# Hybrid decoder layer on Trainium2: chunk matrices of the RWKV-7 mixing as 64-wide quarters, with the loop over head pairs written out

## The reference

```python
def step(st, inp):
    r_t, w_t, k_t, v_t, kk_t, a_t = inp
    sa = jnp.einsum('bhvk,bhk->bhv', st, kk_t)
    st = (st * w_t[:, :, None, :]
          - sa[..., None] * (kk_t * a_t)[:, :, None, :]
          + v_t[..., None] * k_t[:, :, None, :])
    y = jnp.einsum('bhvk,bhk->bhv', st, r_t)
    return st, y
```

## Time and profile before

| | |
|---|---|
| median of 3 runs | 1986.58 us (1986.14 to 1987.74) |
| profiled execution | 1987.96 us, its span 1986.2 us |
| granted TensorE clock, mean | 0.909 |
| TensorE, VectorE, ScalarE, GpSimd busy | 89%, 74%, 54%, 16% of the span |
| DMA | 456.72 MB |

### The profile page before, as it was taken

How to read it: one execution, slowest core, us unless ns; L and a number is a source line. 1 busy time by engine, 2 the same in 40 slices (tenths; PEclk the granted TensorE clock), 3 DMA queues, 4 the chain that set the end, 5 groups by cost and what they waited for, 6 DMA issues and landing times. The chain is left out here.

```text
span 1986.2 us, 26691 instructions
## 1 busy us (share of the span) xinstructions
PE 1771.6 (89%) x8812; PEld 1454.7 (73%) x8813; DVE 1465.4 (74%) x1291; ACT 1063.3 (54%) x979; POOL 308.7 (16%) x206
## 2 busy tenths in 40 slices
PE   6996978868695968999999999999999999999963
PEld 5884756747475856888888888888888888888851
DVE  3225646466664456998999989989989999999845
ACT  4233122122111345777777777777777777777731
POOL 6000000000000000221221222222212212222200
PEclk9997867859687978999999999999999999999985
DMA  5330000000001266999999999999999999999915
GB/s 158 95 96 15 1 1 3 0 3 0 0 0 41 100 240 257 345 363 361 355 363 364 358 369 358 362 369 348 356 370 346 360 367 347 363 359 353 360 69 224
DMA packets 98151, 456.72 MB, mean 230 GB/s; under 512 B 13152, under 2 KB 40816, under 8 KB 48400
## 3 DMA queue, kind: packets, MB, share of 16 engines
q1 hardware_dynamic: 87664, 435.93, 57.8%
q0 software_dynamic: 10464, 20.50, 2.8%
HBM read 452.71 MB, written 20.97 MB: 238 GB/s over the span
## 5 line engine op out<-in xcount | busy, mean ns | idle before, releaser
L1385 DVE TENSOR_TENSOR w_pieces_lo<-w_pieces,w_pieces_hi 128x2048 fp32r<-128x2048 f32 x384 | 870.8, 2288 | 103.8 <-ACT w_pieces_hi L1287 103.7
L1287 ACT ACTIVATE w_pieces_hi<-w_pieces 128x2048 fp32r<-128x2048 f32 x384 | 736.7, 1919 | 310.0 <-PE psum L1535 238.1
L1532 PE MATMUL psum<-w_pieces_hi,xh 128*128 128x512 f32 x1024 | 289.8, 405 | 0.0
L1532 PE MATMUL psum<-w_pieces_hi,xl 128*128 128x512 f32 x1024 | 276.7, 392 | 0.0
L1535 PE MATMUL psum<-w_pieces_lo,xh 128*128 128x512 f32 x1024 | 276.1, 391 | 0.0
L1532 PEld LDWEIGHTS psum<-w_pieces_hi,xl 128*128 128x128 f32 x1024 | 193.4, 189 | 42.7
L1535 PEld LDWEIGHTS psum<-w_pieces_lo,xh 128*128 128x128 f32 x1024 | 192.9, 188 | 42.8
L1532 PEld LDWEIGHTS psum<-w_pieces_hi,xh 128*128 128x128 f32 x1024 | 184.8, 191 | 32.4 <-issue 0.5
L1260 POOL DMA_INDIRECT expert_rows<-ys,this_i x32 | 156.6, 4892 | 282.4 <-ACT ys L1307 282.4
L1552 PE MATMUL psum<-w_pieces_hi,ah 128*128 128x512 f32 x512 | 161.5, 397 | 1.5 <-DVE al L1408 1.5
L1552 PE MATMUL psum<-w_pieces_hi,al 128*128 128x512 f32 x512 | 159.0, 392 | 0.0
(11 more groups left out here) (322 smaller groups left out, 2409.9 us busy)
## 6 DMA issues: line engine op xcount, KB each, us to landing
w_pieces<-in_mlp_w SPq DMA_DIRECT2D x384, 1024.0 KB, 6.4
w_raw<-in_w_in SPq DMA_DIRECT2D x26, 512.0 KB, 4.0
y<-expert_rows SPq DMA_DIRECT2D x3, 2048.0 KB, 14.0
w_pieces<-in_w_out SPq DMA_DIRECT2D x8, 512.0 KB, 9.1
x<-in_x SPq DMA_DIRECT2D x4, 512.0 KB, 6.7
h_rows<-w_pieces POOLq DMA_DIRECT2D x4, 512.0 KB, 2.9
y<-expert_rows SPq DMA_DIRECT2D x4, 512.0 KB, 19.9
out<-x SPq DMA_DIRECT2D x4, 512.0 KB, 2.6
```

What stands on the lines that cost most here:

```text
L1287: nc.scalar.activation(hi[:, p % RING], raw[:, raw_slot(b, p)].rearrange("p r n -> p (r n)"), ACT.Copy).then_inc(s_hi, 1)
L1385: nc.vector.tensor_tensor(lo[:, p % RING], raw[:, raw_slot(b, p)].rearrange("p r n -> p (r n)"), hi[:, p % RING].bitcast(F32), ALU.subtrac ...
L1532: nc.tensor.matmul(bank(c), a[:, k, :], hi[:, p % RING, c * 512:(c + 1) * 512], start=False, stop=False)
```

## The change

- Chunk matrices are stored as 64-wide quarters. A tile's two chunks lie on partitions 0-63 and 64-127, each with 64 columns, with no zeros beside them. `ab`, `ak`, `xx` halve in width, masks too. Each 128x128 product becomes two 64x64 products, one with rows 0-63 to output partitions 0-63, one with rows 64-127 to 64-127. Both halves of one t or x product write the same bank.
- Cross products become 64x64 products over all four combinations of head and half (`quarters`). The b products with kappa are made in both directions, so `xx` is formed in both forms at once by VectorE; the two turns of `xx` and their copies go.
- Beta with r, khat with kappa and r, their masks (`er`, `ek`), the rope's second part, `bonus`, the turns of khat and v and their copies move into the levels. The rope swap goes to banks 7 and 6 and waits for `gate`.
- `akv`, `wu`, `q`, `y_within` and z are on 64-wide parts too, `chunk` and y in an order where neighbours lie on different parts. `gt` is 64 wide; `eg` is one instruction. One more `y_within` stands ahead of the z steps and none after z7; a wait for the new step `y_in` precedes y.
- `am` and `at_` get buffers of their own. The four `Fori` loops become Python loops.

```diff
-        with pe.Fori(0, HEADS) as j:
+        for j in range(HEADS):
...
-            def cross(a, b0, src, h):
-                rows = slice(64 * h, 64 * h + 64)
+            def quarters(part):
                 for t in range(NT):
-                    c0 = (t % 2) * 2 * P
-                    last = nc.tensor.matmul(bank(b0 + t // 2, c0, c0 + 2 * P), src[rows, t * P:(t + 1) * P],
-                                            kr[rows, t, :, :].rearrange("p a c -> p (a c)"), start=True, stop=True)
-                last.then_inc(PE.sem, PE.step(f"m{a}{h}"))
+                    for h in range(2):
+                        for c in range(2):
+                            last = part(h, halves[h], t, c, slice(t * P + c * CH, t * P + (c + 1) * CH))
+                return last
+
+            def toward_kappa(h, dims, t, c, tok):
+                nc.tensor.matmul(bank(h, t * P + CH, (t + 1) * P, halves[c]), beta[dims, tok], kr[dims, t, 0, halves[c]], start=True, stop=True)
...
-            dv("rhat")
-            cross("b", 0, beta, 0)
-            dv("khat")
+            dv("beta")
+            quarters(toward_kappa)
+            quarters(from_kappa).then_inc(PE.sem, PE.step("mb"))
             ac("v_major")
...
             for lv in range(5):
                 for h in range(2):
-                    if lv == 0:
-                        ac(f"x_major{h}")
-                    else:
-                        dv(f"ex{lv - 1}_{h}")
+                    dv(f"ex{lv - 1}_{h}" if lv else f"ea{h}")
                     for t in range(NT):
-                        last = nc.tensor.matmul(bank(4 + h, t * P, t * P + P), ab[:, h, t, 0, :], xx[:, h, t, 0, :], start=True, stop=True)
+                        for c in range(2):
+                            rows = halves[c]
+                            last = nc.tensor.matmul(bank(4 + h, t * CH, (t + 1) * CH, rows), ab[rows, h, t, 0, :], xx[rows, h, t, 0, :],
+                                                    start=True, stop=True)
                     last.then_inc(PE.sem, PE.step(f"t{lv}_{h}"))
-                if not lv:
+                if lv == 0:
+                    dv("khat")
+                    quarters(from_k).then_inc(PE.sem, PE.step("mk"))
+                    ac("e_beta")
+                elif lv == 2:
+                    dv("ek1")
+                    quarters(toward_r).then_inc(PE.sem, PE.step("mr"))
+                elif lv == 3:
+                    dv("er")
+                    turned("t_khat", 0, lambda t: khat[:, t * P:(t + 1) * P])
+                    nc.tensor.matmul(bank(1), con("heads"), r_, start=True, stop=True).then_inc(PE.sem, PE.step("bonus"))
+                elif lv == 4:
                     ac("e_khat")
-                    turned("t_v", 6, lambda t: v_[:, t * P:(t + 1) * P])
+                    turned("t_v", 0, lambda t: v_[:, t * P:(t + 1) * P])
...
             for c in range(1, 7):
                 dv(f"z{c}")
-                nc.tensor.matmul(bank(2, c * 64, c * 64 + 64), gt[:, c, :], zz[:, c, :], start=True, stop=True).then_inc(
-                    PE.sem, PE.step(f"z{c}"))
+                for rows in halves:
+                    last = nc.tensor.matmul(bank(2, c * CH, (c + 1) * CH, rows), gt[rows, c, :], zz[rows, c, :], start=True, stop=True)
+                last.then_inc(PE.sem, PE.step(f"z{c}"))
                 if c < 6:
-                    y_within(c + 1)
+                    last = y_within(c + 2)
...
             dv("z7")
-            y_within(7)
...
+            pe.wait_ge(PE.sem, PE.reached(j, "y_in"))
```

On VectorE, level by level:

```diff
...
                 if lv:
                     weights(lv - 1)
+                else:
+                    rope_turned()
...
+                if lv == 0:
+                    rope_summed()
+                elif lv == 1:
+                    keys_masked()
+                elif lv == 2:
+                    r_masked()
+                elif lv == 3:
+                    bonus()
                 if lv < NT:
                     masked(lv)
```

More of the change, by code:

```diff
@@ L356, in _ @@
                     tile(i * 2 + u, i, u)
[L360 to L364, removed]
@@ L365 @@
-MIX_ACT = (["sig_w", "v_copy", "kk_sq", "sig_a", "kk_norm", "gate", "exps", "v_major", "e_kappa", "x_major0", "e_beta",
-            "x_major1", "e_khat", "e_v"]
-           + [f"{a}{i}" for i in range(NT) for a in ("exp", "a_major", "o_copy")]
+MIX_PE = (["lora_w", "lora_a", "kk_sum", "lora_g", "v_turn", "rope_swap", "mb", "t_kappa", "t_beta"]
+          + ["t0_0", "t0_1", "mk", "x0_0", "x0_1", "score0"]
+          + ["t1_0", "t1_1", "x1_0", "a_turn0", "x1_1", "o0", "score1"]
+          + ["t2_0", "t2_1", "mr", "x2_0", "a_turn1", "x2_1", "o1", "score2"]
+          + ["t3_0", "t3_1", "t_khat", "bonus", "x3_0", "a_turn2", "x3_1", "o2", "score3"]
+          + ["t4_0", "t4_1", "t_v", "x4_0", "a_turn3", "x4_1", "o3"]
+          + ["akv", "o_turn", "wu0", "wu1", "q", "chunk"] + ["z1", "z2", "z3", "z4", "z5", "y_in", "z6", "y", "y_turn"])
@@ L371 @@
-           + [f"{a}{h}" for h in range(2) for a in ("emb", "x1a", "x1b", "emk")] + ["bon"]
-           + [n for lv in range(5) for n in [f"et{lv}_0", f"et{lv}_1"] + [f"{a}{lv - 1}" for a in ("rl", "nl", "p2", "a")] * (lv > 0)
-              + [f"ex{lv}_0", f"ex{lv}_1"] + [f"masked{lv}", f"max{lv}"] * (lv < NT)]
+            "kappa", "b", "beta", "rhat", "am", "kmod", "khat"]
+           + [f"{a}{h}" for h in range(2) for a in ("x1a", "x1b", "ea")]
+           + ["et0_0", "et0_1", "qs", "ks", "rk", "ex0_0", "ex0_1", "q", "k", "masked0", "max0"]
@@ L374 @@
+           + [n for lv in range(1, 5) for n in [f"et{lv}_0", f"et{lv}_1"] + [f"{a}{lv - 1}" for a in ("rl", "nl", "p2", "a")]
+              + [f"ex{lv}_0", f"ex{lv}_1"] + [[], ["ek0", "ek1"], ["er"], ["bon"], []][lv] + [f"masked{lv}", f"max{lv}"] * (lv < NT)]
            + ["o_rs", "o_n", "o_out", "eg", "eh", "e_q"] + [f"z{c}" for c in range(1, 8)]
@@ L792, in _ @@
[L792 to L801 removed]
+            ac("gate")
@@ L832, in _ @@
                     u = h * NT + t
-                    last = nc.tensor.matmul(bank(4, u * 64, u * 64 + 64), ak[:, h, t, 0, :], vt[:, t, 64 * h:64 * h + 64], start=True, stop=True)
+                    for c in range(2):
+                        rows = halves[c]
+                        last = nc.tensor.matmul(bank(4, u * CH, (u + 1) * CH, rows), ak[rows, h, t, 0, :], vt[rows, t, halves[h]],
+                                                start=True, stop=True)
             last.then_inc(PE.sem, PE.step("akv"))
@@ L841, in _ @@
                 for t in range(NT):
[L842 removed]
+                    for c in range(2):
+                        rows = halves[c]
+                        last = nc.tensor.matmul(bank(5 * (1 - h), t * P, t * P + P, rows), xx[rows, h, t, 1, :], rh[rows, h, t, :],
+                                                start=True, stop=True)
                 last.then_inc(PE.sem, PE.step(f"wu{h}"))
@@ L886, in _ @@
+            for t in range(NT):
+                for h, hs, c, tok in each:
+                    last = nc.tensor.matmul(bank(4 + h, t * CH, (t + 1) * CH, tok), qt[hs, t, tok], zz[hs, 2 * t + c, :],
+                                            start=False, stop=t == NT - 1)
             last.then_inc(PE.sem, PE.step("y"))
```

245 lines of the change are left out of this document (130 added, 115 removed).

## The result

The changed kernel takes 1877.5 us (median of 4 runs, 1870.75 to 1877.7) beside 1987.16 before: a ratio of 0.9439 (95% interval 0.9417 to 0.9461), faster by 110 us. I had said 1912 with a range of 1878 to 1948. The direction and the kind of gain in the stretches came out, the size did not: 74 us forecast, 110 measured. The same kernel measured again, as the base of later runs, gave 1872.61 us, 0.9415 (0.9391 to 0.9440).

What follows compares the result with a forecast made beforehand. The mixing block was taken as a chain handed between engines, bound by neither memory nor one engine. Terms 15.5 - 2.0 - 0.3 + 1.1 + 4.3 = 18.6 us a pair, 74 for four, gave 1912 us, range 1878 to 1948.

Steps and rivals of the forecast that it cites:

- price of a pass on four parts: 64x64 passes, q and chunk included: 42 ns each, read from L884 at granted clock 0.50; 27 ns kept as a bound.
- clock in the levels: TensorE's granted clock in the mixing levels, called the large unknown: half the level time taken at full clock, half at low.
- D: Stretch from the first q product to eg (q and chunk), 6.8 us: saving 1.1 a pair, bounds nothing and 3.0.
- A: Stretch from the rope swap to the first score mask, 33.5 us: saving 14.4 to 17.0 a pair, taken 15.5.
- E: Stretch from eg to y_sum, with the z steps: 13.0 to 8.7 us, a saving of 4.3 a pair.
- B: Stretch of four score masks up to akv, 33.3 us: 31.3 at full clock, 39 at low, loss of 2.0 taken.
- C: Stretch from akv to the first q product, 8.2 us, with wu: a loss of 0.3 a pair.
- The paragraph on switching: Changes between 128x128 and 64x64 passes on TensorE: claimed to cost nothing that shows, so no term in the sum.
- The written-out loop: Four loops over pairs written out as new code: costed at nothing, since the first pair took no longer than the period.
- rival 1: The clock stays full through the levels: 24.4 us saved a pair, 1889 us; chance 0.20.
- Rival 3: A level product's two parts, writing the same psum bank, don't overlap: slower, 2031 us; chance 0.06.
- rival 4: TensorE's queue or code is late: 53 ns a 64x64 pass whatever its neighbour; with code bursts 1940 to 1970; chance 0.06.

## Why the prediction was wrong

The chain and the way in which it would shorten were right. Two terms were mis-sized, the price of a pass on four parts and the clock in the levels, and three smaller ones add to them.

- **What bounds the kernel**: right. The block is a chain, what it lost the kernel lost (27.1 a pair, four pairs, 108 of 110 us by these rows).
- **Price of a pass on four parts**: the first step that failed. I took 42 ns from L884 as a measured rate and kept 27 as a bound. The rows of after give 27 to 29 at the low clock, and the base measured again gives 15 at the full one (128 passes of D in 2.23 us less a tail of 0.3). This is 1.9 of the 3.0 in D, 0.9 in A (64 passes) and 0.5 in E, where the y products take 1.13 us instead of 1.61: 3.3 of the 8.5 us that the sum fell short. L884 was a mixture: at 0.50 a pass by itself is 107 ns, two parts give 53, four 27, and 42 lies between two rates. The 53 ns for one part at the full clock was such a mean too: inside a run on one part the starts are 58 ns apart.
- **The clock in the levels**: the second, a term that was mis-sized. I gave half the time to each level of the clock; B ran at 0.86 and A at 0.82. B came to 33.3, against 31.3 forecast for the full clock and 39 for the low one. Its first two steps in the second pair (the other two stand above):

```profile
290.21:296.88 6.67, 6.05 (x109) 4.98 (x107) 5.05 (x13) 1.69 (x8) 0.00 (x0) 0.74 0.01 2
296.88:304.50 7.62, 5.70 (x142) 4.45 (x141) 5.08 (x12) 2.01 (x8) 0.00 (x0) 1.00 0.01 2
```

  So two of four steps ran full and two at about 0.73: 6.7, 7.6, 9.1 and 9.9 us. At the full clock the steps measure 6.2, 7.6, 9.1 and, with the wait filled, 8.2 (forecast 6.8, 7.5, 8.9, 8.1), so the full price held in the sum of the four. Of the low prices only the last step's was met (9.9 for 9.6 forecast); those of 9.9 and 11.6 us for the second and third were not. B is 2.0 us from this. A saved 18.3 us where 17.0 was forecast for the full clock; 1.5 of its 2.8 us is the way from the 15.5 taken to that end, with level 0 at 1.00, 0.9 the price above, and 0.4 isn't traced. The row that spoke for a low clock was read too narrowly: the stretch from 310 to 328 us, taken for products on 64 rows, holds some 4 us of turns on 128 rows too, and the swap ahead of it, on the full array, also ran at 0.50, behind a wait of 4.95 us. How the clock falls differs between pairs, as A's 17.2 and 16.9 us in the base show, so part of this term is luck.
- **C**: forecast as a loss of 0.3, a gain of 0.3. From akv to wu it takes 4.02 us instead of 4.43, most of it in the turn ahead of wu (0.59 us instead of 0.91 to wu's start, at a fuller clock); wu to q takes 3.82 instead of 3.74.
- **The paragraph on switching**: its reading was wrong. It took the start of L884 ahead of a modelled end for no cost. But a pass that waits for nothing always starts ahead of that end; what counts is by how much. Before, then after, around a change of size:

```profile
395.64 0.69 PE L866 MATMUL psum<-vt,ak 128*128 128x64 f32 x2 [0.38 <-DVE zz L693]
396.13 0.63 PE L867 MATMUL psum<-wu,ab 128*128 128x64 f32 x2
396.69 1.61 PE L884 MATMUL psum<-zz,t 64*64 64x64 f32 x32
```
```profile
301.87 0.28 PE L858 MATMUL psum<-t,xx 64*64 64x64 f32 x4
301.99 0.28 PE L862 MATMUL psum<-xx,t 64*64 64x64 f32 x4
302.20 0.71 PE L780 MATMUL psum<-vm,at 128*128 128x128 f32 x4
```

  In one size the next group starts 0.20 us ahead of the end at the low clock (396.13 against 396.33) and 0.16 at the full one (301.99 against 302.15). At a change it starts 0.07 ahead at either, and so at every change in the second pair of both kernels that waits for nothing. A change of size thus costs some 0.14 us at the low clock and 0.09 at the full one. The sum had no term for it; it works against the gain and doesn't explain the miss, and how much of it lies on the path isn't shown.
- **The moved steps**: right in kind. The levels had room for them: under 0.1 us of cost in the first two at equal clock, against 6.6 of gain ahead. In the run that undid them the third level lost its full-array products and its full clock together, a use I hadn't seen and which stays argued.
- **wu, z, y**: z steps are 0.72 us apart at the full clock and 0.87 at the low one, for the 0.8 forecast. eg is 0.7 us shorter, as forecast.
- **The written-out loop**: put at nothing, worth 0.7 a pair; code fetched anew cost nothing that shows.
- **The rivals**: the measured time lies below rival 1 too (the full clock, 1889), although the clock wasn't full, since that case kept the 42 ns in D and A and had nothing for the loop. Rival 3, no overlap in one bank, is refuted, and so is rival 4, 53 ns a pass whatever its neighbour. The range failed because its lower end took the bound of D alone: rival 1 with that bound is 26.3 us a pair, 1881 us, and the range went to 1878; the same bound in A and E would have made it 1876. The price, the clock, C, the loop and what isn't traced in A (3.3, 3.5, 0.6, 0.7 and 0.4 us a pair) make up the 8.5.

## What to carry to other kernels

When small products are laid on neighbouring parts of the array, their order decides as much as their size: at the full clock the same q and chunk products take 6.53 us in runs of one part and 2.23 in rotation, and runs of one part in the levels cost 27 us here, a good part of it with a lower clock. Take a pass price from a stream whose pattern is that of the new one, and price one, two and four parts apart; a mean over a mixed stream is none of them. Where TensorE has waits, look at the granted clock of the stretch behind them. Two products nobody reads, sized to fit inside the wait, gave 12 to 16 us here by the ratios (0.9357 against 0.9415 and 0.9439). Four gave part of it back, and filling further waits brought nothing more.

## What the runs showed of the hardware

- 64x64 parts (rows 0-63 to partitions 0-63, rows 64-127 to partitions 64-127) that write one bank overlap fully: 29 ns a pass at a granted clock of 1.00, 53 at 0.50, where one part alone gives 58 and 107. Four parts give 15 and 27 ns. The Trainium skill, TensorEngine Tiling (Array Packing), Gotcha 1: PSUM Pressure, would have had them wait for each other; the trace doesn't agree where they write different halves of the partitions.
- A float32 pass of 512 columns on 128x128 costs 427 ns at the full clock.
- A change between 128x128 and 64x64 passes costs 0.09 us at a granted clock of 1.00 and 0.14 at 0.50, against passes of one size.
- The granted clock of a stretch of identical work was 1.00 in one pair and 0.51 in another of the same execution, and moved the stretch from 2.23 to 3.83 us. What decides it between pairs stays open.
